# Late second-table gathers, a last batch in two parts, and whole output quarters in one transfer

## The chip, the core and the metric

The kernel runs on one core of a Trainium2 chip. A core has TensorE (PE, matmul; PEld is its weight load), VectorE (DVE), ScalarE (ACT), GpSimd (POOL) and SyncE (SP), each with its own instruction stream, and 16 DMA engines that they share. PE writes its results to eight banks. The metric is the device time of one execution in microseconds, as the median of a few runs.

## The reference

Two transformer blocks run over 256 tokens of width 2048. The change touches only the end of the second one, a layer of 16384 single-neuron experts that are picked by product keys. For each token and each of 8 heads, 16 experts are chosen by two sorted key searches; `expert_u` and `expert_v` are the two tables of 16384 rows of 2048 floats.

```python
def token_block(args):
    xb, idx, g = args
    u = jnp.take(expert_u, idx, axis=0)
    a = jnp.einsum('thkd,td->thk', u, xb)
    hid = jax.nn.gelu(a) * g
    vsel = jnp.take(expert_v, idx, axis=0)
    return jnp.einsum('thk,thkd->td', hid, vsel)

x = x + peer(rms_norm_2(x, norm2_g[l]), ...)   # token_block over blocks of 128 tokens
```

## The kernel before

Everything up to the expert layer is left alone by the change. In the expert layer the tokens are two tiles of 128. Experts whose first key is 88 or more are computed densely from whole panels, which are all used up by about 2930 us. The others are gathered row by row with indirect DMAs: a gather moves, for one slot of one head, a row of 2048 floats for each of 128 tokens, and leaves out tokens whose expert is a dense one. There are 256 gathers from the first table (u0 to u255, line 585) and 256 from the second (v0 to v255, line 601). Four consecutive gathers of each make one of 64 batches g; batches 32 to 63 belong to the second tile.

What a batch goes through, engine by engine:

- POOL issues all gathers, in program order, in the loop at line 608. First-table rows go to one of 5 buffers `u_slot` (`gather_u` waits for the dot that read the buffer five gathers ago, `dot_ready`), second-table rows to one of 7 buffers `v_slot` (`gather_v` waits for the matmuls of the gather seven before it, `v_used`). In step k the loop issues u(k) and then v(k-4); after u255 it issues v252 to v255.
- DVE takes the dot product of a gathered row and the token in two halves (`dot`, line 1706), adds the halves of a batch (`dots_summed`, line 1718), and later multiplies gelu by the gate (`hidden`, line 1756). In the loop at line 1798 `hidden(g - 1)` stands behind the first dot of batch g.
- ACT takes gelu of a batch (line 1097) and then spreads the four products of every token into 16 blocks of 32 x 32, four for each of the four second-table gathers (`spreads`, line 1050), which are the weights of PE's next matmuls.
- PE takes, for each second-table gather k, its spread and its rows and adds into one of the four banks of a tile (`adds`, line 2291): a quarter q of the tile's 32 x 4 block. It waits for `spread_ready` and for the gather's landing. The last batch, 63, finishes one quarter with each of its four gathers and signals `acc_done`.
- DVE copies a finished quarter from its bank to `out_row` (`result`, line 1796): the first tile's four quarters at the end of batch 61, the second tile's four at the very end.
- SP sends `out_row` to HBM (line 484). A quarter lies as 128 partitions of 512 floats, and partitions c*32 to c*32+31 are columns c*512 and on of 32 output rows. SP sends it as four transfers of 32 partitions.

Of the kernel before, what the change touches and what calls it, by code (L numbers as in the profile page):

```python
# [24 lines left out]
TT = T // 128  # L25
# [8 lines left out]
PH, TOPK, NKEYS = 8, 16, 128  # L34
SLOTS = PH * TOPK
# [90 lines left out]
SHRINK = 2.0 ** -16  # L126
# [43 lines left out]
def v_panels_in(i):  # L170

    return range(3 * (i - 34) // 2, min(DENSE, 3 * (i - 33) // 2)) if i >= 34 and 3 * (i - 34) // 2 < DENSE else range(0)


class Counts:
# [39 lines left out]
def two_layers(nc, stream, dense_u, columns, x, meta, b_out, g_mix_post, g_ffn, g_ffn_post, g_norm1, g_norm2, w_forget,  # L215
               forget_bias, group_w, keys, expert_u, expert_v, out):
    f32, f32r, u32 = mybir.dt.float32, mybir.dt.float32r, mybir.dt.uint32
    ACT, ALU, AX = mybir.ActivationFunctionType, mybir.AluOpType, mybir.AxisListType


    K, Q = 1024, 32
# [17 lines left out]
    ident = keep("s_ident", [128, 128])  # L239
# [87 lines left out]
    NU, NV, NW, NH, BATCH, LAG = 5, 7, 4, 4, 4, 4  # L327
    ROUTES, GROUPS = TT * PH, TOPK // BATCH
# [10 lines left out]
    out_row = place("s_out_row", [128, TT, D], S + 24 * K)  # L339
# [43 lines left out]
    with ExitStack() as ctx:  # L383
# [68 lines left out]
        @block.sync  # L452
        def _(sp):
            sp.dma_start(meta_sb[:, :], meta).then_inc(meta_loaded, 16)
            for t in range(TT):
                sp.dma_start(xres[:, t, :], x[t * 128:(t + 1) * 128, :]).then_inc(x_loaded[t], 16)
            sp.dma_start(cols[:, :], columns).then_inc(cols_loaded, 16)
            for s in range(4):
                sp.dma_start(raw[s][:, :], stream[s]).then_inc(raw_loaded[s], 16)
            panels = stream.rearrange("(q s) p n -> q s p n", s=4)  # L460
            with sp.Fori(1, NPANELS // 4) as q:
                for s in range(4):


                    sp.wait_ge(panel_used, q * 4 + (s - 4 + 1 + 1))
                    sp.dma_start(raw[s][:, :], panels[bass.ds(q, 1), s].rearrange("a p n -> (a p) n"))\
                        .then_inc(raw_loaded[s], 16)
            for d in range(NE, 2 * DENSE):
                if d == DENSE:
                    sp.wait_ge(panel_used, NPANELS + 1 + DENSE)  # L470
                    sp.dma_start(xn_late[:, :], put_by[0]).then_inc(xn_back, 16)
                    sp.dma_start(xres_late[:, :], put_by[1]).then_inc(xres_back, 16)
                if d < NE + 2:
                    sp.wait_ge(split_ready, NSPLITS - 3 + d - NE)
                else:
                    sp.wait_ge(panel_used, NPANELS + 1 + d + 1 - 2)
                src = dense_u[d] if d < DENSE else expert_v[(SPARSE + d - DENSE) * NKEYS:(SPARSE + d - DENSE + 1) * NKEYS, :]
                r = (d - NE) % 2
                sp.dma_start(raw[r][:, :], src).then_inc(raw_loaded[r], 16)
            for t in range(TT):  # L480
                for q in range(4):
                    sp.wait_ge(out_ready, 4 * t + q + 1)
                    for c in range(4):
                        sp.dma_start(out[t * 128 + q * Q:t * 128 + (q + 1) * Q, c * 512:(c + 1) * 512],
                                     out_row[c * Q:(c + 1) * Q, t, q * 512:(q + 1) * 512]).then_inc(stored, 16)
            sp.wait_ge(stored, 16 * 16 * TT)


        @block.gpsimd
        def _(pool):  # L490
            n = Counts()
# [112 lines left out]
            gather_u(0)  # L604
            gather_v(0)
            gather_v(1)
            for k in range(1, ROUTES * TOPK + LAG):
                if k < ROUTES * TOPK:
                    gather_u(k)
                for first in {4: (2, 3), 5: (4, 5), 6: (6,)}.get(k, ()):  # L610
                    gather_v(first)
                if k >= LAG + NV:
                    gather_v(k - LAG)


        @block.scalar
        def _(act):
# [420 lines left out]
            v_indices(2)  # L1038


            def spreads(g):

                act.wait_ge(hid_ready, g + 1)
                if g == 0:
                    act.wait_ge(panel_used, NPANELS + 1 + 1)
                wait(act, v_used, 4 * (g + 1 - NW))
                for q in range(4):
                    for s in range(4):
                        own = slice(q * Q, (q + 1) * Q)
                        ins = act.activation(spread[g % NW][s * Q:(s + 1) * Q, q, :], ident[own, own], ACT.Copy,  # L1050
                                             scale=hid[g % NH][own, s:s + 1])
                    ins.then_inc(spread_ready, 1)

            def dense_hidden(d):

# [29 lines left out]
            for g in range(ROUTES * GROUPS):  # L1085
                if g == 18:
                    for t in range(TT):
                        slots_transposed(t)
                if g:
                    spreads(g - 1)  # L1090
                    for d in u_panels_in(g - 1):
                        dense_hidden(d)
                for f in token_fours_in(g):
                    if f % 4 < 2:
                        one_keys(f)
                act.wait_ge(dots_added, g + 1)
                act.activation(gelu[g % NH][:, :], adot[g % NH][:, :], ACT.Gelu_apprx_tanh, scale=1.0 / SHRINK).then_inc(gelu_ready, 1)
                if route_in(g):
                    gate_exps(route_in(g))
                    v_indices(route_in(g))  # L1100
            spreads(ROUTES * GROUPS - 1)


        @block.vector
        def _(dve):
# [603 lines left out]
                                                   accum_out=halfdot[g % NH][:, h * BATCH + s:h * BATCH + s + 1])  # L1709
                ins.then_inc(dot_ready, 1)  # L1710

            def dots_summed(g):

                dve.wait_ge(dot_ready, (g + 1) * BATCH)
                if g >= NH:
                    dve.wait_ge(gelu_ready, g - NH + 1)
                two = halfdot[g % NH]
                dve.tensor_tensor(adot[g % NH][:, :], two[:, 0:BATCH], two[:, BATCH:], ALU.add).then_inc(dots_added, 1)

            def one_keys_2(m):  # L1720

# [27 lines left out]
                dve.tensor_tensor(some, some, bank[b][:, 0:GATE_TOKENS * DENSE].rearrange("p (t g) -> p g t", t=GATE_TOKENS), ALU.mult)\  # L1749
                    .then_inc(bank_empty[b], 1)  # L1750

            def hidden(g):

                th, j = four_of(g)
                dve.wait_ge(gelu_ready, g + 1)
                dve.tensor_tensor(hid[g % NH][:, :], gelu[g % NH][:, :], gate_kept[th][:, j * BATCH:(j + 1) * BATCH], ALU.mult)\  # L1756
                    .then_inc(hid_ready, 1)


            dve.wait_ge(iota_ready, 1)  # L1760
# [32 lines left out]
            def result(t, q):  # L1793

                dve.wait_ge(acc_done, 4 * t + q + 1)
                dve.tensor_copy(out_row[:, t, q * 512:(q + 1) * 512], bank[4 * t + q][:, :]).then_inc(out_ready, 1)

            for g in range(ROUTES * GROUPS):
                for turn in range(BATCH):
                    dot(g * BATCH + turn)  # L1800
                    if turn == 0 and g:
                        hidden(g - 1)
                        if route_in(g - 1):
                            gates_softmax(route_in(g - 1))
# [9 lines left out]
                            one_keys_late(f // 4)  # L1814
                    if g == 32 and turn < 2:
                        gated(T // GATE_TOKENS - 2 + turn)
                dots_summed(g)
                if g == 61:
                    for q in range(4):
                        result(0, q)  # L1820
            hidden(ROUTES * GROUPS - 1)
            for q in range(4):
                result(1, q)

# [575 lines left out]
```

## Time and profile before

| | us |
|---|---|
| median of three runs | 3002.79 |
| lowest and highest | 2999.24, 3002.88 |
| the profiled execution | 3000.82 |
| its span | 2998.8 |
| PE busy | 2758.8 |
| DVE busy | 1923.8 |
| ACT busy | 1178.2 |
| POOL busy | 652.6 |

The span runs from the first to the last instruction of the profiled execution; about 2 us of that execution's time lie outside it. The page's forty slices are 75 us each. Views of the trace name an operation by its line, its engine and its tiles, and give the idle time before it in brackets with what ended it. The chain of waits is followed back from the last instruction, at each step to what released it.

### The profile page before, as it was taken

Reading aid. Unit: us, or ns where it says so; the run is one execution under the profiler, and the core shown is the slowest. Engines: PE = TensorE matmul, PEld = TensorE weight load, DVE = VectorE, ACT = ScalarE, POOL = GpSimd, SP = SyncE. Lnnn points to the kernel's source line nnn. Section 1 sums busy time; section 2 is a strip of 40 time slices with the busy share of each in tenths; the row PEclk is TensorE's granted clock in tenths of the full one; section 3 lists DMA queues with packets and bytes.
Section 4 is the critical chain, followed back from the end, with each engine's and each line's share of the span. In section 5 each row is a group of like instructions: output and inputs, shape, how many; then the busy total and the mean of one; then the engine's idle time right before and its main releaser. Section 6 shows DMA issues by size and latency. Waiting matters only on the chain.

```text
span 2998.8 us, 45605 instructions
## 1 busy us (share of the span) xinstructions
PE 2758.8 (92%) x17100; PEld 2069.8 (69%) x17100; DVE 1923.8 (64%) x3184; ACT 1178.2 (39%) x2298; POOL 652.6 (22%) x568
## 2 busy tenths in 40 slices
PE   8999999999999997999999999999977887887884
PEld 7886788888888887989999889777754432222230
DVE  6888566556656565455444558987869875555555
ACT  1003443333334344435334444655556542222223
POOL 0000000000000000040000002444447664444453
PEclk9999999999999998999999999999977678998996
DMA  6333545555555553443455657999999999999998
GB/s 244 141 141 106 206 161 187 184 194 182 191 187 187 190 184 129 155 155 141 177 186 184 239 200 259 363 418 409 416 383 396 390 416 417 415 413 394 414 407 319
DMA packets 131299, 785.52 MB, mean 262 GB/s; under 512 B 34631, under 2 KB 34631, under 8 KB 35847
## 3 DMA queue, kind: packets, MB, share of 16 engines
q1 hardware_dynamic: 55424, 393.68, 35.6%
q0 software_dynamic: 75712, 389.74, 32.3%
q8 instruction: 94, 1.54, 0.2%
q14 instruction: 69, 0.56, 0.1%
HBM read 940.23 MB, written 4.19 MB: 315 GB/s over the span
## 4 chain that ended last, share of the span: by engine, by line
PE 57%; DMA 19%; DVE 12%; issue 7%; ACT 3%; POOL 2%; DVEq 1%; POOLq 0%; SPq 0%; ACTq 0%
DMA s_u<-in_expert_u,s_u_index 15%; PE bank L1847 10%; PE bank L1841 10%; PE bank L1842 10%; PE bank L1843 10%; PE bank L1848 5%; PE bank L1937 4%; PE bank L2240 4%; DVE s_u L1706 4%; DMA s_v<-in_expert_v,s_v_index 3%; PE bank L2291 2%; POOL s_u L585 2%; DVE s_cacc L1217 2%; DVE s_w_lo L1128 1%; DVE s_yrow L1390 1%
## 5 line engine op out<-in xcount | busy, mean ns | idle before, releaser
L1128 DVE TENSOR_TENSOR s_w_lo<-s_raw,s_w_hi 128x2048 fp32r<-128x2048 f32 x258 | 592.6, 2297 | 578.0 <-ACT s_w_hi L628 577.6
L628 ACT ACTIVATE s_w_hi<-s_raw 128x2048 fp32r<-128x2048 f32 x256 | 490.4, 1916 | 751.7 <-PE bank L1843 476.3
L1847 PE MATMUL bank<-s_a,s_w_hi 128*128 128x512 f32 x1408 | 493.8, 394 | 3.4 <-DVE s_w_lo L1128 3.2
L1706 DVE CUSTOM_DVE_ANT_0 s_u<-s_u,s_xn_late 128x1024 f32<-128x1024 f32 x256 | 303.7, 1224 | 244.0 <-DMA s_u<-in_expert_u,s_u_index 217.1
L2291 PE MATMUL bank<-s_v,s_spread 128*32 128x512 f32 x2048 | 310.3, 715 | 152.0 <-DMA s_v<-in_expert_v,s_v_index 121.6
L1050 ACT ACTIVATE s_spread<-s_ident,s_hid 32x32 f32<-32x32 f32 x1024 | 325.7, 318 | 205.0 <-DVE s_hid L1756 175.8
L1848 PE MATMUL bank<-s_a,s_w_lo 128*128 128x256 f32 x1408 | 394.8, 280 | 0.0
L585 POOL DMA_INDIRECT s_u<-in_expert_u,s_u_index x256 | 292.5, 1142 | 432.1 <-DVE s_halfdot L1706 267.9
L601 POOL DMA_INDIRECT s_v<-in_expert_v,s_v_index x256 | 309.9, 1211 | 191.7 <-PE bank L2291 109.6
L1706 DVE CUSTOM_DVE_ANT_0 s_u<-s_u,s_xn 128x1024 f32<-128x1024 f32 x256 | 303.8, 1224 | 56.0 <-DMA s_u<-in_expert_u,s_u_index 49.6
L1841 PE MATMUL bank<-s_a,s_w_hi 128*128 128x256 f32 x1152 | 325.3, 282 | 4.1 <-DVE s_a L1152 2.4
L1842 PE MATMUL bank<-s_a,s_w_hi 128*128 128x256 f32 x1152 | 324.6, 282 | 0.0
L1843 PE MATMUL bank<-s_a,s_w_lo 128*128 128x256 f32 x1152 | 324.2, 281 | 0.0
L1847 PEld LDWEIGHTS bank<-s_a,s_w_hi 128*128 128x128 f32 x1408 | 264.3, 188 | 66.5 <-DVE s_w_lo L1128 6.4
L2291 PEld LDWEIGHTS bank<-s_v,s_spread 128*32 128x32 f32 x2048 | 64.1, 119 | 345.0 <-issue 267.0
L2250 PE MATMUL bank<-s_raw,s_ha 128*32 128x512 f32 x2560 | 298.9, 616 | 0.2 <-DMA s_raw<-in_expert_v 0.2
L2240 PE MATMUL bank<-s_xnt,s_raw 128*128 128x256 f32 x1184 | 264.8, 382 | 2.9 <-ACT s_ha L1060 1.7
L1848 PEld LDWEIGHTS bank<-s_a,s_w_lo 128*128 128x128 f32 x1408 | 264.6, 188 | 0.4
L2240 PEld LDWEIGHTS bank<-s_xnt,s_raw 128*128 128x128 f32 x1184 | 222.1, 190 | 59.6 <-issue 28.2
L1937 PE MATMUL bank<-s_a_f,s_raw 128*128 128x272 f32 x1024 | 235.2, 393 | 2.1 <-DVE s_a_f L1185 1.4
L2250 PEld LDWEIGHTS bank<-s_raw,s_ha 128*32 128x32 f32 x2560 | 97.6, 115 | 201.6 <-issue 195.7
L1841 PEld LDWEIGHTS bank<-s_a,s_w_hi 128*128 128x128 f32 x1152 | 218.0, 189 | 8.5 <-issue 4.4
(321 smaller groups left out, 3821.8 us busy)
## 6 DMA issues: line engine op xcount, KB each, us to landing
s_raw<-in_stream SPq DMA_DIRECT2D x292, 1024.0 KB, 4.7
s_raw<-in_expert_v SPq DMA_DIRECT2D x40, 1024.0 KB
s_raw<-in_dense_u SPq DMA_DIRECT2D x37, 1024.0 KB
s_u<-in_expert_u,s_u_index POOLq DMA_INDIRECT x256
s_v<-in_expert_v,s_v_index POOLq DMA_INDIRECT x256
s_panel_early<-in_dense_u POOLq DMA_DIRECT2D x3, 1024.0 KB, 11.4
s_xres<-in_x SPq DMA_DIRECT2D x2, 1024.0 KB, 5.9
out<-s_out_row SPq DMA_DIRECT2D x32, 64.0 KB
```

The lines of the kernel that those rows point to most:

```text
L628: act.activation(w_hi[s % 2][:, :], raw[s][:, :], ACT.Copy).then_inc(hi_ready, 1)
L1128: dve.tensor_tensor(w_lo[s % 2][:, :], raw[s][:, :], w_hi[s % 2][:, :].bitcast(f32), ALU.subtract)\
L1706: ins = dve.tensor_tensor_reduce(out=u_slot[k % NU][:, half], in0=u_slot[k % NU][:, half], in1=xn_late[:, half] if t else xn[:, 0, half], ...
L1841: pe.matmul(dst, left[0], right[0], start=start, stop=False)
L1842: pe.matmul(dst, left[0], right[1], start=False, stop=False)
L1843: return pe.matmul(dst, left[1], right[0], start=False, stop=stop)
L1847: pe.matmul(dst, left[0], both, start=start, stop=False)
L1848: return pe.matmul(dst[:, 0:T], left[1], both[:, 0], start=False, stop=stop)
L1937: ins = pe.matmul(bank[c][:, 0:L], raw[c % 4][:, k * 128:(k + 1) * 128], a_f[:, k, :], start=k == 0, stop=k == KT - 1)
L2240: ins = pe.matmul(bank[b][:, 0:T], source[:, k * 128:(k + 1) * 128], xnt[:, k, 0:T], start=k == 0, stop=k == KT - 1)
L2250: ins = pe.matmul(bank[4 * t + q][c * Q:(c + 1) * Q, :], ha[:, d, t * 128 + q * Q:t * 128 + (q + 1) * Q], raw[r][:, c * 512:(c + 1) * 512] ...
L2291: ins = pe.matmul(bank[4 * t + q][c * Q:(c + 1) * Q, :], spread[g % NW][:, q, :], v_slot[k % NV][:, c * 512:(c + 1) * 512], start=False, s ...
```

## The change

Three things change. First, POOL's loop: up to step 247 it stays at u(k), v(k-4). In steps 248 to 255 a second-table gather is issued only in every second step (`v_steps_in`), so v244, v245 and v246 follow u249, u251 and u253, and v247 to v255 all follow u255. Second, the last batch: `hidden(62)` stands ahead of the first dot of batch 63 instead of behind it. The sum, gelu and product of batch 63 are made for its first three slots before the last dot and for the fourth after it, and its 16 spread blocks come as twelve and then four; `spread_ready` is signalled with the last four. Third, SP sends an output quarter as one transfer instead of four, with the 4 x 32 x 512 arrangement on the HBM side.

```diff
+def v_steps_in(k):
+    if k < SLOTS * TT - 8:
+        return range(k - 4, k - 3)
+    first = SLOTS * TT - 12 + (k - SLOTS * TT + 8) // 2
+    if k == SLOTS * TT - 1:
+        return range(first, SLOTS * TT)
+    return range(first, first + k % 2)
...
-                    for c in range(4):
-                        sp.dma_start(out[t * 128 + q * Q:t * 128 + (q + 1) * Q, c * 512:(c + 1) * 512],
-                                     out_row[c * Q:(c + 1) * Q, t, q * 512:(q + 1) * 512]).then_inc(stored, 16)
-            sp.wait_ge(stored, 16 * 16 * TT)
+                    sp.dma_start(out[t * 128 + q * Q:t * 128 + (q + 1) * Q, :].rearrange("p (c n) -> c p n", c=4),
+                                 out_row[:, t, q * 512:(q + 1) * 512]).then_inc(stored, 16)
+            sp.wait_ge(stored, 16 * 4 * TT)
...
-            for k in range(1, ROUTES * TOPK + LAG):
-                if k < ROUTES * TOPK:
-                    gather_u(k)
+            for k in range(1, ROUTES * TOPK):
+                gather_u(k)
...
-                if k >= LAG + NV:
-                    gather_v(k - LAG)
+                for own in v_steps_in(k):
+                    if own >= NV:
+                        gather_v(own)
...
+            def last_spreads(g):
+                act.wait_ge(hid_ready, g + 1)
+                act.wait_ge(v_used, 4 * (g + 1 - NW))
+                for q in range(4):
+                    for s in range(3):
+                        one_spread(g, q, s)
+                act.wait_ge(dots_added, g + 2)
+                gelu_of(g, slice(3, 4))
+                act.wait_ge(hid_ready, g + 2)
+                for q in range(4):
+                    one_spread(g, q, 3).then_inc(spread_ready, 1)
...
-                act.activation(gelu[g % NH][:, :], adot[g % NH][:, :], ACT.Gelu_apprx_tanh, scale=1.0 / SHRINK).then_inc(gelu_ready, 1)
+                gelu_of(g, slice(0, 3 if g == ROUTES * GROUPS - 1 else 4))
...
-            spreads(ROUTES * GROUPS - 1)
+            last_spreads(ROUTES * GROUPS - 1)
...
+            last = ROUTES * GROUPS - 1
             for g in range(ROUTES * GROUPS):
+                if g == last:
+                    hidden(g - 1)
                 for turn in range(BATCH):
+                    if g == last and turn == 3:
+                        dots_summed(g, 0, 3)
+                        hidden(g, 0, 3)
                     dot(g * BATCH + turn)
-                    if turn == 0 and g:
+                    if turn == 0 and 0 < g < last:
                         hidden(g - 1)
...
-                dots_summed(g)
+                if g == last:
+                    dots_summed(g, 3, 4)
+                else:
+                    dots_summed(g)
...
-            hidden(ROUTES * GROUPS - 1)
+            hidden(last, 3, 4)
```

On POOL the last twelve gathers stand as follows, before and then now. `s_u_133` to `s_u_137` are the five first-table buffers, `s_v_138` to `s_v_144` the seven second-table buffers, and the number behind an index names the head.

```order
L585 DMA s_u_135<-in_expert_u,s_u_index_190 128x2048
L601 DMA s_v_141<-in_expert_v,s_v_index_205 128x2048
L585 DMA s_u_136<-in_expert_u,s_u_index_190 128x2048
L601 DMA s_v_142<-in_expert_v,s_v_index_205 128x2048
L585 DMA s_u_137<-in_expert_u,s_u_index_190 128x2048
L601 DMA s_v_143<-in_expert_v,s_v_index_205 128x2048
L585 DMA s_u_133<-in_expert_u,s_u_index_190 128x2048
L601 DMA s_v_144<-in_expert_v,s_v_index_205 128x2048
L601 DMA s_v_138<-in_expert_v,s_v_index_206 128x2048
L601 DMA s_v_139<-in_expert_v,s_v_index_206 128x2048
L601 DMA s_v_140<-in_expert_v,s_v_index_206 128x2048
L601 DMA s_v_141<-in_expert_v,s_v_index_206 128x2048
```

```order
L610 DMA s_v_139<-in_expert_v,s_v_index_204 128x2048
L594 DMA s_u_137<-in_expert_u,s_u_index_190 128x2048
L594 DMA s_u_133<-in_expert_u,s_u_index_190 128x2048
L610 DMA s_v_140<-in_expert_v,s_v_index_204 128x2048
L610 DMA s_v_141<-in_expert_v,s_v_index_205 128x2048
L610 DMA s_v_142<-in_expert_v,s_v_index_205 128x2048
L610 DMA s_v_143<-in_expert_v,s_v_index_205 128x2048
L610 DMA s_v_144<-in_expert_v,s_v_index_205 128x2048
L610 DMA s_v_138<-in_expert_v,s_v_index_206 128x2048
L610 DMA s_v_139<-in_expert_v,s_v_index_206 128x2048
L610 DMA s_v_140<-in_expert_v,s_v_index_206 128x2048
L610 DMA s_v_141<-in_expert_v,s_v_index_206 128x2048
```

Before, u252 to u255 alternate with v248 to v251 and four second-table gathers follow; now nine follow u255 (`s_u_133`, index 190), from v247 to v255.

On DVE the end of batch 63 stands as follows, before and then now. An ISA row that writes `s_u` is half a dot, one with `s_halfdot` alone reads its sum.

```order
L1706 ISA s_u_137,s_halfdot_226<-s_u_137,s_xn_late 128x1024
L1706 ISA s_halfdot_226 128x1
L1706 ISA s_u_133,s_halfdot_226<-s_u_133,s_xn_late 128x1024
L1706 ISA s_halfdot_226 128x1
L1706 ISA s_u_133,s_halfdot_226<-s_u_133,s_xn_late 128x1024
L1706 ISA s_halfdot_226 128x1
L1718 TENSOR_TENSOR s_adot_230<-s_halfdot_226 128x4
L1756 TENSOR_TENSOR s_hid_238<-s_gelu_234,s_gate_kept_222 128x4
L1796 COPY s_out_row<-bank 128x512 x4
```

```order
L1748 TENSOR_TENSOR s_adot_230<-s_halfdot_226 128x3
L1787 TENSOR_TENSOR s_hid_238<-s_gelu_234,s_gate_kept_222 128x3
L1736 ISA s_u_133,s_halfdot_226<-s_u_133,s_xn_late 128x1024
L1736 ISA s_halfdot_226 128x1
L1736 ISA s_u_133,s_halfdot_226<-s_u_133,s_xn_late 128x1024
L1736 ISA s_halfdot_226 128x1
L1748 TENSOR_TENSOR s_adot_230<-s_halfdot_226 128x1
L1787 TENSOR_TENSOR s_hid_238<-s_gelu_234,s_gate_kept_222 128x1
L1827 COPY s_out_row<-bank 128x512 x4
```

The sum and the product are made twice, for three slots ahead of the last dot and for one behind it; the four copies stay last.

On SP the end of the program, the last panel loads and the output, stands as follows, before and then now.

```order
L479 DMA s_raw_65<-in_expert_v 128x2048
L479 DMA s_raw_66<-in_expert_v 128x2048
L479 DMA s_raw_65<-in_expert_v 128x2048
L484 DMA out<-s_out_row 32x512 x32
L383 UNCONDITIONAL_BRANCH
```

```order
L489 DMA s_raw_65<-in_expert_v 128x2048
L489 DMA s_raw_66<-in_expert_v 128x2048
L489 DMA s_raw_65<-in_expert_v 128x2048
L493 DMA out<-s_out_row 4x32x512 x8
L393 UNCONDITIONAL_BRANCH
```

Thirty-two transfers of the form 32x512 become eight of the form 4x32x512, in the same place.

## Rows read from the trace of the kernel before

**Rows 1.** The page's forty slices: DMA busy tenths and GB/s.

```profile
DMA  6333545555555553443455657999999999999998
GB/s 244 141 141 106 206 161 187 184 194 182 191 187 187 190 184 129 155 155 141 177 186 184 239 200 259 363 418 409 416 383 396 390 416 417 415 413 394 414 407 319
```

**Rows 2.** Chain of waits, last 50 us: start us, us, what.

```profile
2950.33 19.74 DMA s_u<-in_expert_u,s_u_index
...
2973.95 1.98 PE bank L2291 x8
...
2976.76 14.89 DMA s_v<-in_expert_v,s_v_index
...
2991.79 1.10 PE bank L2291 x8
...
2992.91 0.69 DVE s_out_row L1796
```

**Rows 3.** Busy us by stretch, engine by engine (instructions); last: PEclk, DMA share, GB/s.

```profile
2936.00:2976.00 40.00, 17.40 (x76) 2.17 (x80) 25.48 (x49) 13.85 (x45) 19.47 (x18) 0.54 1.00 404
...
2976.00:2980.00 4.00, 1.54 (x12) 0.19 (x8) 2.38 (x4) 1.82 (x6) 0.99 (x1) 0.92 0.76 279
2980.00:2984.00 4.00, 1.35 (x8) 0.00 (x0) 2.24 (x3) 0.00 (x0) 0.00 (x0) 0.51 0.31 129
2984.00:2988.00 4.00, 3.76 (x20) 0.73 (x24) 0.46 (x4) 3.26 (x11) 0.00 (x0) 0.50 0.06 27
```

**Rows 4.** DMA view of 2984:2988, all packets.

```profile
DMA packets 20, 0.11 MB, mean 27 GB/s; under 512 B 7, under 2 KB 7, under 8 KB 7
```

**Rows 5.** Timeline of DVE, batches 62 and 63: start us, us, what [idle before].

```profile
2965.37 1.23 DVE L1706 CUSTOM_DVE_ANT_0 s_u<-s_u,s_xn_late 128x1024 f32<-128x1024 f32 x1 [2.60 <-issue]
...
2970.09 1.23 DVE L1706 CUSTOM_DVE_ANT_0 s_u<-s_u,s_xn_late 128x1024 f32<-128x1024 f32 x1 [2.14 <-DMA s_u<-in_expert_u,s_u_index]
...
2972.39 0.16 DVE L1756 TENSOR_TENSOR s_hid<-s_gelu,s_gate_kept 128x4 f32<-128x4 f32 x1
...
2977.50 1.23 DVE L1706 CUSTOM_DVE_ANT_0 s_u<-s_u,s_xn_late 128x1024 f32<-128x1024 f32 x1 [1.67 <-DMA s_u<-in_expert_u,s_u_index]
...
2981.76 1.23 DVE L1706 CUSTOM_DVE_ANT_0 s_u<-s_u,s_xn_late 128x1024 f32<-128x1024 f32 x1 [1.88 <-DMA s_u<-in_expert_u,s_u_index]
```

**Rows 6.** Timeline of POOL: the issues of u255 and of v255.

```profile
2963.61 0.99 POOL L585 DMA_INDIRECT s_u<-in_expert_u,s_u_index  x1 [2.57 <-DVE s_halfdot L1706]
...
2976.76 0.99 POOL L601 DMA_INDIRECT s_v<-in_expert_v,s_v_index  x1 [4.58 <-PE bank L2291]
```

**Rows 7.** Timeline of ACT (gelu of batch 62) and of PE (matmuls of v251 to v255).

```profile
2967.99 0.20 ACT L1097 ACTIVATE s_gelu<-s_adot 128x4 f32<-128x4 f32 x1 [8.21 <-DVE s_adot L1718]
...
2984.08 1.93 PE L2291 MATMUL bank<-s_v,s_spread 128*32 128x512 f32 x8 [2.74 <-DMA s_v<-in_expert_v,s_v_index]
2986.17 4.82 PE L2291 MATMUL bank<-s_v,s_spread 128*32 128x512 f32 x24 [0.15 <-ACT s_spread L1050]
2991.79 1.06 PE L2291 MATMUL bank<-s_v,s_spread 128*32 128x512 f32 x8 [0.80 <-DMA s_v<-in_expert_v,s_v_index]
```

**Rows 8.** Timeline of SP, the second tile's output, and of DVE, its first copy.

```profile
2988.17 0.69 DVE L1796 COPY s_out_row<-bank 128x512 f32<-128x512 f32 x1 [3.41 <-PE bank L2291]
2988.89 8.21 SPq L484 DMA_DIRECT2D out<-s_out_row  x16
```

**Rows 9.** DMA view, output queue q1: first tile in 2952:2968, second in 2989.6:2999 (with slices).

```profile
q1 hardware_dynamic: 768, 1.05, 17.7%
...
DMA  4510055540918172919191818281918281810000
...
q1 hardware_dynamic: 768, 1.05, 42.4%
```

## What I expected, written before the run

> **What bounds the kernel now.** I read the page's slices first, then the chain of waits at the end, then short stretches. From about 1900 us to the end the DMA engines are busy throughout (mean share 0.8 to 0.9 and more, 360 to 418 GB/s but for the last slice) [rows 1]. The chain of waits ends with the last second-table gather: POOL issues v255 at 2976.76, it lands 14.89 us later, then come one set of matmuls, one copy and the output [rows 2]. Taken at its word, the chain says that v255 was issued too late, because its slot waited for the matmuls at 2973.95, and these for a first-table landing at 2970.07 [rows 2].
>
> The stretches say otherwise. From 2936 to 2976 the share is 1.00 at 404 GB/s, so the 16 engines move about 25 GB/s each, while PE is busy for 17.4 of the 40 us. It falls to 0.31 in 2980:2984 and to 0.06 in 2984:2988, where 27 GB/s are left [rows 3, 4]. A share of 0.06 is one engine of 16, still at its full rate. The other fifteen drained at about 2981: 0.31 x 16 x 4 us is 19.8 us of engine time, less 4 for the one, over 15. So one engine is some 10 us behind the others, and every gather waits for its part.
>
> Was that engine ever out of work near the end? When POOL issued u255 at 2963.61, u251 had not been consumed (its dot starts at 2965.37); when it issued v255 at 2976.76, the dots of u254 (2977.50) and u255 (2981.76) had not begun [rows 5, 6]. Issues ran ahead of that engine's landings all the time. So the landing at 2991.66 follows from how many rows the slowest engine has to move, and not from when v255 was issued.
>
> **The change part by part.**
>
> *Order of the gathers.* The same 512 gathers are issued. Eight move: v244 now follows u249 instead of u248, v245 to v247 pass 2, 3 and 4 first-table gathers, v248 to v250 pass 3, 2 and 1, v251 none. On the slowest engine this exchanges places in a queue that does not run dry, so v255's landing changes by 0. The new wait is POOL's: after u255 come nine second-table gathers, and v253 to v255 wait for the matmuls of v246 to v248. Behind a waiting gather stand only the rest of the nine, and PE waits for them. The cover is the queue: when v246 lands, u254, u255 and v247 to v252 are still to come. Eight gathers at 1.9 us (v251's matmuls start at 2984.08, v255 lands at 2991.66, four gathers between [rows 2, 7]) are some 15 us against about 1 us of POOL for an issue [rows 6]. Each microsecond without this cover would cost one at the end. I take 0.
>
> *Last batch in two parts.* Batch 62's product now comes ahead of dot 252. Gelu is ready at 2968.19, the product was made at 2972.39 behind a dot that waited for its row until 2970.09 [rows 5, 7], so it comes 4.2 us earlier. Batch 63's spreads were late: PE's 24 matmuls at 2986.17 were released by ACT [rows 7]. With u255 four places further ahead (4 x 1.9 = 7.6 us) they are ready before v252 lands. Then PE takes each gather as it lands; but v255's matmuls waited for the DMA already (0.80 us idle [rows 7]), so the gain on the path is 0. ACT gets one gelu more and DVE a sum and a product more (0.16 to 0.20 us each) plus two waits for gelu; they stand before dots 252 and 255, far ahead of v252. A loss is possible: PE's eight matmuls took 1.06 us at the end, but 1.93 in sparser work [rows 7], so up to +0.9.
>
> *Output.* This is where the sum is made. Before, each quarter (128 x 512) went out in four transfers of 32 rows of 2 KB. SP issued the last 16 in 8.21 us, 0.51 each, until 2997.10, though the last copy ended at 2993.60 [rows 2, 8]. So 3.5 us of SP's issuing lie on the path. Now there are four issues, and that term goes. What is late next is the transfer itself. SP's row gives the old form as 32x512 and the new one as 4x32x512; every other SP row in this program has 128 outermost, or 16. The old form used more than a quarter of the engines: its packets filled 42.4% of 16 engines [rows 9]. No row shows an outermost count of 4. The bounds: its 128 rows go over 16 engines, 8 each, or over 4, one per outermost index, 32 each. I take four, since a share per outermost index is what the form asks for.
>
> A sentence of the Trainium skill stands behind this: "DMA: Bandwidth & Descriptors", section "Why a DMA increments its semaphore by 16 and not by 1", says that the outermost dimensions of both sides set how many engines take part, the largest count up to 16 that divides both. By that rule 4 and 128 give four engines, and on SP's queue always the same four. No run here shows it yet.
>
> Price of a 2 KB row on one engine: in 2952:2968, between gathers, 512 of them took 17.7% of 16 x 16 us, so 0.088 us; at the end 42.4% of 16 x 9.4 us, so 0.125 [rows 9]. I take 0.088, the price with work queued, and keep 0.125. A quarter is then 32 x 0.088 = 2.8 us on four engines, the second tile's four quarters 11.3 us. The first tile's quarters, at about 2950, put 128 rows on each of the four instead of 32 (+8.5 us) and take 2.8 us from each of the other twelve.
>
> *Sum*, slowest engine among the twelve: last gather 2991.66 - 2.8 = 2988.8. v252 lands three gathers sooner, 2983.1; matmuls 1.9, copy 0.7, issue and start about 1: the first quarter's packets begin at 2986.8, and 11.3 us of them end at 2998.1. The four engines' own work gives 2981 + 8.5 + 11.3 = 3000.8, or 2998.0 if the 2.8 us by which the queue runs sooner count in full. I take 2999.0 for the last packet. The last slices before the end are empty, 0.9 us [rows 9], so the span is 2999.9: **1.1 us over the 2998.8 profiled**. That execution took 3000.82 in all; the median of the three runs is 3002.79 (2999.24 to 3002.88). So 3003.9. At 0.125 the burst is 16 us: +5.8, 3008.6.
>
> **The rivals.**
>
> *All sixteen engines.* The first tile's load is spread as before, the last gather lands at 2991.66, the last copy ends at 2993.60, the issue at 2994.1; from the end of the last issue to the end of the span it was 1.7 us, plus six more rows per engine at 0.088 to 0.125, 0.6: 2996.4, which is -2.4, and 3000.4. For it: all transfers of before spread widely. Against: none had this form.
>
> *The chain is right.* If the landing follows the issue, batch 62's product 4.2 us earlier brings v255 4.2 us earlier, with the 2.4 above -6.6: 2996.2. Against: rows 3 to 6.
>
> *The slowest engine is one of the four* (the slower side). Its gathers then end 8.5 us later, 3000.2, and the first three quarters' rows alternate with its last gathers, up to 8.5 more; after that matmuls, copy, issue, 2.8 of rows and 0.9: about 7. The middle is 3011.4, +12.6, so 3015.4 (3011.2 to 3019.7). It decides as soon as the four include that engine, one case in four when four engines are used. No row names the engine.
>
> *The merge saves SP nothing*, if an issue of the new form takes four times as long: the page has no such row; 16 x 0.51 would be kept at most, and the time stays at 3002.8. I count it with the forecast.
>
> **How the numbers follow.** Four engines 0.62: 0.47 without the slowest engine (forecast 3003.9) and 0.15 with it. Sixteen engines 0.30. The chain right 0.08. Range: 2997 to 3009 holds the forecast with its dearer row and the sixteen engines with the spread of the runs, and leaves out 0.15 above and about half of 0.08 below. What a measurement of this kernel can tell from no change is about 0.2%, 6 us: faster 0.05 (the chain right, in part), slower 0.16, the same 0.79.
>
> **What would show it.** The first table's last dot some 7 us earlier against the last second-table landing, nine second-table issues in a row on POOL, and a landing of v255 that is not earlier for being issued otherwise: the order is worth nothing. Four SP issues in the last stretch instead of 16. Over the last 9 us the output queue's share at 25% of the engines or under, near 4 x 25 GB/s, with packets back to back: four engines; short bursts above 25% and an end about 3 us after the last copy: sixteen. v255 landing near 2988.8: the first tile's rows left the slowest engine; after 2999: they fell on it. I am wrong in the main step if v255 lands much earlier without that, with DMA share 1.00 until later than 2977, and wrong on the price if a quarter takes far from 2.8 us.

## The result and the profile after

| | before | after |
|---|---|---|
| median, us (runs) | 3002.19 (22) | 3005.70 (22) |
| lowest and highest | 2999.12, 3004.93 | 3003.55, 3009.69 |
| ratio, 95% interval | | 1.0014 [1.0008, 1.0019] |
| the profiled execution | 3000.82 | 3004.03 |
| its span | 2998.8 | 3002.0 |

The changed kernel is 3.5 us slower, 0.14%. The forecast of 3003.9 had the direction and 1.1 us of it. The span of the profiled execution grew by 3.2 us. The stretches of the kernel after (busy us by engine, then PEclk, DMA share, GB/s) answer [rows 3]:

```profile
2944.00:2948.00 4.00, 1.93 (x8) 0.23 (x8) 3.02 (x7) 0.00 (x0) 1.69 (x2) 0.50 0.80 299
2948.00:2952.00 4.00, 1.93 (x8) 0.23 (x8) 3.97 (x8) 0.21 (x1) 1.27 (x2) 0.50 0.89 323
2952.00:2956.00 4.00, 1.08 (x8) 0.20 (x8) 3.80 (x9) 2.35 (x8) 1.41 (x2) 0.50 0.73 261
...
2980.00:2984.00 4.00, 3.87 (x24) 0.58 (x16) 0.00 (x0) 0.00 (x0) 0.98 (x1) 0.65 0.90 336
2984.00:2988.00 4.00, 2.38 (x20) 0.37 (x16) 0.99 (x2) 0.00 (x0) 0.00 (x0) 1.00 0.38 154
2988.00:2992.00 4.00, 2.13 (x16) 0.37 (x16) 1.78 (x3) 0.00 (x0) 0.00 (x0) 1.00 0.24 67
2992.00:2996.00 4.00, 0.00 (x0) 0.00 (x0) 0.00 (x0) 0.00 (x0) 0.00 (x0) 0.63 0.26 102
2996.00:3000.00 4.00, 0.00 (x0) 0.00 (x0) 0.00 (x0) 0.00 (x0) 0.00 (x0) 0.50 0.26 100
```

Read it from below. The last 8 us hold nothing but the output, at a share of 0.26 and 100 GB/s: four engines of 16, at 25 GB/s each. Further up, two things changed places. In 2944 to 2956, where the DMA engines had been full [rows 3], the share is 0.73 to 0.89; and in 2980:2984, where before only a third of the engines had work, it is 0.90. Most engines now have gaps in the middle and work to do at the end.

The end of the chain of waits (start us, us, what) answers [rows 2]:

```profile
2957.11 11.61 DMA s_u<-in_expert_u,s_u_index
...
2980.39 9.44 DMA s_v<-in_expert_v,s_v_index
...
2989.96 1.10 PE bank L2331 x8
...
2991.09 0.69 DVE s_out_row L1827
```

v255 is issued 3.6 us later than before and lands at 2989.83 (2980.39 + 9.44), 1.8 us earlier. The last copy ends at 2991.78, but the span at 3002.0. The view of what SP waits for (line, releaser: us, times, longest) and the DMA view of 2989.6 to 3002 (slices of 0.31 us in tenths and in GB/s, then the output queue: packets, MB, share) say what fills those 10.2 us:

```profile
SPq L393 <- DMA out<-s_out_row: 9.2, 1, 9.2
```

```profile
DMA  1322222222222222222222222222222221000000
GB/s 66 53 53 79 73 86 92 106 99 106 106 92 99 106 106 99 106 106 106 92 99 106 106 99 106 106 92 99 106 106 99 106 86 59 20 26 26 13 0 0
...
q1 hardware_dynamic: 514, 1.02, 22.2%
```

SP has issued everything and waits 9.2 us for the stores. The rows run back to back, at some 100 GB/s, where before they came in bursts with pauses [rows 9]. One of them costs 0.222 x 16 x 12.4 / 514 = 0.086 us.

### The profile page after: what moved, and what is told of

Same layout as the page of the kernel before. It is cut to its first block, busy times and chain, and to the rows that moved or that the text cites. A ratio compares the mean times of both kernels' runs of the same rounds, so it can differ in the third digit from the quotient of the medians.

```text
span 3002.0 us, 45585 instructions
## 1 busy us (share of the span) xinstructions
PE 2760.0 (92%) x17100; PEld 2068.9 (69%) x17100; DVE 1924.1 (64%) x3186; ACT 1178.3 (39%) x2299; POOL 657.1 (22%) x568
## 3 DMA queue, kind: packets, MB, share of 16 engines
q8 instruction: 94, 1.54, 0.2%
## 4 chain that ended last, share of the span: by engine, by line
PE 57%; DMA 19%; DVE 11%; issue 7%; ACT 3%; POOL 2%; DVEq 1%; POOLq 0%; SPq 0%; ACTq 0%
DMA s_u<-in_expert_u,s_u_index 15%; PE bank L1887 10%; PE bank L1881 10%; PE bank L1882 10%; PE bank L1883 10%; PE bank L1888 5%; DMA s_v<-in_expert_v,s_v_index 4%; PE bank L1977 4%; DVE s_u L1736 3%; PE bank L2280 3%; PE bank L2331 2%; DVE s_cacc L1247 2%; POOL s_u L594 1%; DVE s_w_lo L1158 1%; PE bank L2320 1%
## 5 line engine op out<-in xcount | busy, mean ns | idle before, releaser
L1887 PEld LDWEIGHTS bank<-s_a,s_w_hi 128*128 128x128 f32 x1408 | 264.3, 188 | 66.4 <-DVE s_w_lo L1158 6.4
L1977 PEld LDWEIGHTS bank<-s_a_f,s_raw 128*128 128x128 f32 x1024 | 194.4, 190 | 43.0 <-issue 3.1
```

The lines of the kernel that those rows point to most:

```text
L1887: pe.matmul(dst, left[0], both, start=start, stop=False)
L1977: ins = pe.matmul(bank[c][:, 0:L], raw[c % 4][:, k * 128:(k + 1) * 128], a_f[:, k, :], start=k == 0, stop=k == KT - 1)
```

## A common mark

Executions drift by up to some 4 us before the end, more than is to be explained. So I compare kernels from a mark that the change leaves in place: the start of the first tile's four copies on DVE, which stands between 2948.1 and 2952.7 in the kernels below. The timelines of DVE have it, of before and after:

```profile
2934.79 1.23 DVE L1706 CUSTOM_DVE_ANT_0 s_u<-s_u,s_xn_late 128x1024 f32<-128x1024 f32 x1 [1.73 <-DMA s_u<-in_expert_u,s_u_index]
...
2949.59 2.48 DVE L1796 COPY s_out_row<-bank 128x512 f32<-128x512 f32 x4
```

```profile
2933.87 1.22 DVE L1736 CUSTOM_DVE_ANT_0 s_u<-s_u,s_xn_late 128x1024 f32<-128x1024 f32 x1 [1.74 <-DMA s_u<-in_expert_u,s_u_index]
...
2948.67 2.48 DVE L1827 COPY s_out_row<-bank 128x512 f32<-128x512 f32 x4
```

A dot that waited for its row stands 14.80 us ahead of the copies in both, so the mark is sound. From it v255 lands at +42.06 before and at +41.16 after (2989.83 - 2948.67). All kernels, in us. Each experiment has 11 runs (the two halves 5), and its ratio is to runs of the kernel before that were taken beside it (medians 3002.86, 3002.81 and 3001.86), not to 3002.19. The last three columns come from one profile each:

| kernel | median | ratio to before [95%] | v255 lands, from the mark | last copy's end to span's end | span's end, from the mark |
|---|---|---|---|---|---|
| before | 3002.19 | | 42.1 | 5.2 | 49.2 |
| after | 3005.70 | 1.0014 [1.0008, 1.0019] | 41.2 | 10.2 | 53.3 |
| output as before | 3000.50 | 0.9997 [0.9988, 1.0006] | 42.7 | 3.5 | 49.0 |
| merged output alone | 3004.75 | 1.0005 [0.9996, 1.0014] | 39.3 | 9.4 | 50.7 |
| first tile merged | 3001.24 | 0.9998 [0.9989, 1.0007] | 41.7 | 5.4 | 49.1 |
| second tile merged | 3005.30 | 1.0009 [1.0000, 1.0018] | 42.7 | 8.7 | 54.0 |
| 128 outermost | 2999.98 | 0.9989 [0.9980, 0.9998] | 43.3 | 2.9 | 48.2 |
| two halves | 3026.21 | 1.0080 [1.0066, 1.0094] | 45.1 | 25.1 | 73.0 |
| two queues | 2999.12 | 0.9989 [0.9980, 0.9998] | 42.6 | 2.9 | 47.4 |
| two queues, old order, old last batch | 2996.86 | 0.9980 [0.9971, 0.9989] | 39.4 | 2.9 | 44.3 |
| two queues, late order alone | 2999.29 | 0.9991 [0.9982, 1.0000] | 42.4 | 2.9 | 47.2 |
| two queues, split last batch alone | 2997.01 | 0.9981 [0.9972, 0.9990] | 39.4 | 3.0 | 44.3 |
| two queues, no first-tile stores | 2996.82 | 0.9981 [0.9972, 0.9990] | 39.6 | 2.9 | 44.4 |

## Experiments: which part costs the time

**The output as before.** The merged transfer is undone in the kernel after:

```diff
-sp.dma_start(out[...].rearrange("p (c n) -> c p n", c=4), out_row[:, t, ...])
+for c in range(4):
+    sp.dma_start(out[..., c * 512:(c + 1) * 512], out_row[c * Q:(c + 1) * Q, t, ...])
```

> The kernel after, with the output as before: 16 transfers of 32x512 for each tile. Left of the change are the order of the late gathers and the last batch in two parts. My theory (one lagging DMA engine sets the end, so the order is worth nothing, and only the merged output made the kernel after 3.5 us longer): the same time as before within 1 us, about 3002, a ratio of 1.000; v255 is issued some 3.6 us later than before and lands within 1 us of 2991.7. Rival (the order holds the last landing back, or brings it forward): v255's landing moves with its issue. If the order or the two parts cost the 3.5 us, this kernel is as long as the one after, about 3005.7; if the chain of waits was right about the issue, it is about 4 us shorter than before, 2998.

The ratio is 0.9997, so the loss is gone with the merged output. In the chain v255 is issued at 2980.41, 3.65 us later than before (4.2 from the mark), and lands at 2991.80, 0.1 us later (0.7 from the mark):

```profile
2980.41 11.39 DMA s_v<-in_expert_v,s_v_index
```

A landing does not follow its issue here: the chain's story of a gather issued too late is refuted, as the forecast said.

**The merged output alone**, on the kernel before:

> The kernel before, with the merged output alone: each quarter one transfer of 4x32x512. My theory (the merged transfer runs on four of the 16 DMA engines and makes all of the loss): as long as the kernel after, +2 to +4 us over before, 3004 to 3006; the last 11 to 13 us at a share of about a quarter of the DMA engines and 100 GB/s. Rival (the order and the two parts make the loss): the same as before or up to 2.4 us shorter, since SP's 3.5 us of issuing go.

The ratio is 1.0005; the interval reaches from none to all of the loss of the kernel after, so the traces must decide. From the mark v255 lands 2.7 us sooner than before, as priced (2.8). The mark, v255 in the chain, and the stretches of this kernel's end:

```profile
2949.33 2.48 DVE L1795 COPY s_out_row<-bank 128x512 f32<-128x512 f32 x4
```

```profile
2973.84 14.83 DMA s_v<-in_expert_v,s_v_index
```

```profile
2980.00:2984.00 4.00, 2.68 (x12) 0.43 (x16) 1.55 (x6) 2.23 (x8) 0.00 (x0) 0.50 0.27 110
...
2992.00:2996.00 4.00, 0.00 (x0) 0.00 (x0) 0.00 (x0) 0.00 (x0) 0.00 (x0) 0.70 0.26 101
```

The four-engine burst is here too, but in 2980:2984 the other engines are through, as before. Its span is 3000.0. The forecast's sum, which put 0 on the other two parts, was 2999.9. From the mark it loses 1.5 us (50.7 against 49.2), where the sum had 1.1. So the sum holds for this part alone, and the kernel after loses 2.6 us more (53.3 against 50.7). The merged output doesn't make all of the loss, as had been expected here, and the parts do not add up. Alone, the late order and the split batch lose nothing at the end (49.0 against 49.2).

**One tile merged, the other not**, both on the kernel after:

```diff
+if t == 0:   # in the other kernel: t == 1
     sp.dma_start(out[...].rearrange("p (c n) -> c p n", c=4), out_row[:, t, ...])
+else:
+    for c in range(4): ...
```

> The kernel after, but only the first tile's quarters are merged; the second tile's go out in four transfers each, as before. My theory: the four DMA engines that carry the merged rows are not the lagging one, so at about 2950 they take 2.8 us of rows from the lagging engine and v255 lands 1 to 2.8 us earlier than before, about 2989 to 2990.5; the end is that of before less that much: a ratio of 0.999 to 0.9997. Rival (the lagging engine is one of the four): v255 lands some 8 us later and the kernel is about 8 us longer. Rival (the first tile's rows matter to nothing): the same as before.

> The kernel after, but only the second tile's quarters are merged; the first tile's go out in four transfers each, as before. My theory (the loss is the burst of 512 rows on four DMA engines at the end, about 13 us from the first packet): v255 lands as before, within 1 us of 2991.7, the first packets come at about 2989, the end at about 3002: +2 to +4 us over before, 3004.5 to 3006.5. If the kernel after also loses by the first tile's rows (they hold back the four engines, so the burst starts behind their gathers), this kernel is some 1 to 3 us shorter than the kernel after. Rival (the second tile's merge is harmless): the same as before.

With the second tile merged alone the end is as late as in the kernel after (54.0 against 53.3 from the mark): the burst is the loss, and the first tile's merge neither adds to it nor takes much away. With the first tile alone v255 gains only 1.0 us over the output as before, not the 2.7 that the same merge gains with the old order. Nor does the end come 1 to 2.8 us sooner, as had been expected (49.1 against 49.2 before): the last landings come closer together, and SP's 16 issues are the tail again. Timelines of SP, of the kernel with the first tile merged and of the one with two queues (below):

```profile
2986.82 8.74 SPq L498 DMA_DIRECT2D out<-s_out_row  x16
```

```profile
2987.86 6.36 SPq L498 DMA_DIRECT2D out<-s_out_row  x8
```

The first ends at 2995.56, 3.65 us after the last copy; the second, with ACT issuing the other half, 0.8 us after it.

## Experiments: how many engines a transfer gets

**A count of 128 outermost, and a count of 2.**

```diff
-out[t * 128 + q * Q:t * 128 + (q + 1) * Q, :].rearrange("p (c n) -> c p n", c=4)
+out.rearrange("t (c n) -> (t c) n", c=4)[(4 * t + q) * 128:(4 * t + q + 1) * 128, :]
```

> The kernel after, still with one transfer for a quarter, but as a plain 128x512 transfer whose outermost count is 128: the same bytes in the same 2 KB rows, written to other places of the output (a quarter's 128 rows of 512 lie one behind the other, so the output's arrangement is not the reference's). My theory: it runs on all 16 DMA engines, so nothing is left of the long burst and SP's issuing tail is gone as well: the output ends about 3 us after the last copy, and the kernel is 2 to 3 us shorter than before, 2999 to 3000, and 5 to 6 us shorter than the kernel after. Rival (one merged transfer costs the time whatever its outermost count, because it starts late or its rows are slow): the same as the kernel after, about 3005.7.

```diff
-sp.dma_start(out[...].rearrange("p (c n) -> c p n", c=4), out_row[:, t, ...])
+for h in range(2):
+    sp.dma_start(out[..., h * 1024:(h + 1) * 1024].rearrange("p (c n) -> c p n", c=2),
+                 out_row[h * 64:(h + 1) * 64, t, ...])
```

> The kernel after, with each quarter in two transfers of 2x32x512 in place of one of 4x32x512. My theory (the outermost count of 4 is what puts the rows on four engines): a count of 2 puts them on two, 64 rows for each transfer's half of a quarter's 128 per engine, 256 rows for a tile: 256 x 0.084 = 21.5 us. The first tile's rows then make these two engines the last ones (2981 + 18.8 = 2999.8), v255 lands at about 2999 or later, and the end is at about 3021 to 3025: +20 to +26 us over before; the share of the DMA engines at the end is 0.13 and about 50 GB/s. Rival (four engines by something else than the outermost count, as the number of rows or the queue): as the kernel after, +3.5, at a share of 0.25.

The DMA view of the plain transfers, 2992 to 2998.6 (slices of 0.165 us):

```profile
DMA  1049995000029998100000000002999700000000
GB/s 50 0 186 410 447 385 211 0 25 37 25 87 385 410 397 323 37 25 25 12 0 0 0 0 0 0 0 112 410 397 397 273 0 0 0 0 0 0 0 0
```

and the stretches of the two halves:

```profile
3000.00:3004.00 4.00, 0.00 (x0) 0.00 (x0) 0.00 (x0) 0.00 (x0) 0.00 (x0) 0.50 0.13 51
3004.00:3008.00 4.00, 0.00 (x0) 0.00 (x0) 0.00 (x0) 0.00 (x0) 0.00 (x0) 0.50 0.13 51
```

The same 2 KB rows run at 400 GB/s with 128 outermost (a quarter takes some 0.8 us), at 100 with 4, and at 51 with 2: all engines, four, two. The output's tail after the last copy is 2.9, 10.2 and 25.1 us. By the Trainium skill ("DMA: Bandwidth & Descriptors", section "Why a DMA increments its semaphore by 16 and not by 1") the outermost dimensions of both sides set the number, as the largest count up to 16 that divides both; these three kernels agree with it. One number of the expectation failed: with two engines v255 was to land at 2999 or later and landed at 2993.85, so the first tile's rows held the gathers back by far less than their 18.8 us. The end held: +23.4 us, a span of 3021.8.

## Experiments: what the late order costs

**Two queues**: the kernel after, with the first tile merged, and the second tile's transfers of 32x512 shared by SP and ACT.

```diff
+for c in range(2):       # SP, second tile
+    sp.dma_start(out[..., c * 512:(c + 1) * 512], out_row[c * Q:(c + 1) * Q, 1, ...])
...
+for q in range(4):       # ACT, behind its last spreads
+    act.wait_ge(out_ready, 4 + q + 1)
+    for c in range(2, 4): act.dma_start(out[..., c * 512:(c + 1) * 512], out_row[c * Q:(c + 1) * Q, 1, ...])
```

> The kernel after, with the first tile's quarters merged and the second tile's in transfers of 32x512 again, of which SP issues two for each quarter and ACT, which is idle by then, the other two. My theory: the first tile's rows leave the lagging engine, v255 lands 1 to 2.8 us earlier than before (2989 to 2990.5); the rows of the end run on all 16 engines; each of the two queues issues 8 transfers of 0.5 us beside the other, so the issuing ends about 1 us after the last copy and the span about 3.3 us after it: 3 to 4 us shorter than before, 2998.5 to 3000, and 1 to 2 us shorter than with SP alone. Rival (the issuing was no limit, or ACT's issues cost more than SP's): the same as with SP alone, 1 to 2 us shorter than before.

**The same output on the kernel before:**

> The kernel before, with the output alone as in the experiment with two queues: the first tile's quarters merged, the second tile's in transfers of 32x512, two of each quarter from SP and two from ACT. Order of the gathers and last batch are those of before. My theory (order and last batch are worth nothing): within 1 us of the experiment with two queues on top of the kernel after, 2998.5 to 3000; v255 is issued some 3 us earlier than there and lands at the same time. It can lose up to 1 us where ACT's spreads, which stand before its issues, release three gathers' matmuls at once. Rival (the order or the last batch is worth something once the output is off the path): 2 us or more apart.

The tail is 2.9 us in both, and the first came to the time expected, though v255 landed only at 2991.47 (0.5 us later than before, from the mark). But the kernel with the old order ends 3.1 us sooner from the mark, and its v255 lands 3.2 us sooner (39.4 against 42.6). "Order and last batch are worth nothing" failed. The mark and v255 with the old order, on DVE's timeline and in the chain:

```profile
2948.14 2.48 DVE L1805 COPY s_out_row<-bank 128x512 f32<-128x512 f32 x4
```

```profile
2972.64 14.89 DMA s_v<-in_expert_v,s_v_index
```

The next two kernels separate the two parts, and a third takes the first tile's stores away. The first diff sets POOL's loop in the one kernel against that in the other; the comments say which last batch each has.

```diff
-for k in range(1, ROUTES * TOPK + LAG):   # old order, split last batch
+for k in range(1, ROUTES * TOPK):         # late order, old last batch
```

> The kernel before with the two-queue output (first tile's quarters merged, second tile's 32x512 transfers shared by SP and ACT), and with the late order of the gathers alone; the last batch is that of before. Measured from the start of the first tile's copies, v255 landed at +39.4 us with the old order and this output, at +42.6 with both the late order and the split last batch. My theory (the late order leaves 15 engines short of work in 2940 to 2960, so they end some 3 us later, and the four that carry the first tile's merged rows become the last): v255 lands at +41 to +43, the share of the DMA engines falls under 0.9 in 2944 to 2956 and is near 0.9 still in 2980 to 2984; the time is 2 to 3 us over that of the old order, 2998.5 to 3000. Rival (the split last batch cost it): v255 at +39.4 and 2996.9.

> The same two-queue output with the old order of the gathers, and the last batch in two parts as the only other change. My theory (the split is worth nothing on the path): v255 lands at +39.4 us after the start of the first tile's copies, as with the unsplit batch, and the time is within 1 us of that, 2996 to 2998. Rival (the split batch cost the time): v255 at +41 to +43 and 2998.5 to 3000. If the three quarters before the last go out earlier and this counts, it is up to 1 us shorter.

```diff
-if t == 0: sp.dma_start(...)   # first tile's stores
```

> The kernel after with the two-queue output for the second tile, and without the stores of the first tile (its half of the output is not written). The late order and the split batch stay. My theory (with the late order the four engines of the first tile's merged rows set the last landings; the lagging engine alone would be ready earlier): without those rows v255 lands at +39 to +40.5 us after the start of the first tile's copies, 2 to 3 us earlier than with them (+42.6), and the time is about 2997. Rival (the late order loses on the lagging engine itself, which runs dry): v255 stays at +41.5 to +43, and the time at 2999.

The copies on DVE's timeline and v255 in the chain, first of the late order alone, then of the kernel without the first tile's stores:

```profile
2949.89 2.48 DVE L1815 COPY s_out_row<-bank 128x512 f32<-128x512 f32 x4
```

```profile
2980.78 11.50 DMA s_v<-in_expert_v,s_v_index
```

```profile
2952.68 2.48 DVE L1834 COPY s_out_row<-bank 128x512 f32<-128x512 f32 x4
```

```profile
2980.85 11.40 DMA s_v<-in_expert_v,s_v_index
```

All three came out as the theory said. The split batch is worth nothing (+39.40; 2997.0 against 2996.9 us). The late order alone costs 3.0 us (+42.39). Without the first tile's stores, the late order costs nothing (+39.57). So the merged first tile loses nothing by itself, and the late order at most the 0.7 us seen with the output as before; together they lose 3.0. The stretches show the link, of the late order and of the old one, both with two queues:

```profile
2952.00:2960.00 8.00, 1.94 (x8) 0.20 (x8) 7.75 (x15) 5.01 (x16) 3.24 (x3) 0.50 0.80 291
2980.00:2984.00 4.00, 2.96 (x16) 0.42 (x16) 0.00 (x0) 0.59 (x2) 0.99 (x1) 0.76 0.94 341
2984.00:2988.00 4.00, 2.67 (x16) 0.65 (x16) 0.00 (x0) 0.00 (x0) 0.00 (x0) 0.67 0.43 175
```

```profile
2952.00:2960.00 8.00, 3.71 (x20) 0.73 (x24) 5.71 (x11) 5.09 (x16) 5.08 (x4) 0.68 0.96 364
2980.00:2984.00 4.00, 3.85 (x20) 0.73 (x24) 0.34 (x4) 3.39 (x11) 0.00 (x0) 0.50 0.24 101
```

With the late order DVE is busy for 7.75 of 8 us in 2952:2960: first-table rows arrive one behind the other, and its dots and the four copies fill it. POOL's next first-table gather waits for a dot, and there is no second-table gather between to issue. On the timeline of POOL that wait, for u253, stands here, first in the late order alone and then in the old order:

```profile
2955.51 1.23 POOL L599 DMA_INDIRECT s_u<-in_expert_u,s_u_index  x1 [3.89 <-DVE s_halfdot L1725]
```

```profile
2953.76 1.70 POOL L589 DMA_INDIRECT s_u<-in_expert_u,s_u_index  x1 [2.59 <-DVE s_halfdot L1715]
```

u253 goes out 5.62 us behind the mark in both, so the late order doesn't bring the first table's rows forward here. By then the old order has also issued v246, v247 and v248, and the late order none of them: those are the rows that the engines miss.

So the share falls to 0.80, and the work that the engines miss then comes at the end, at 0.94 in 2980:2984 where the old order has 0.24. The lagging engine hardly cares (0.7 us with the output as before), since it has a queue throughout. But the others used to be some 10 us ahead of it, and now have less: v255 is their last work too, and is issued some 4 us later, which leaves about 6 (an estimate). The first tile's merged rows put 8.5 us more on four of them, by the forecast's price. With 10 us to spare that is hidden, with 6 it is not.

The trace settles which engine ended last. It keeps sixteen landing signals for a gather, as many as there are DMA engines. Those of v255 in order of time, in us from the mark, and the time from v254's last signal to v255's:

| kernel | ninth | 13th, 14th, 15th | last | from v254's last |
|---|---|---|---|---|
| before | 31.8 | 32.1, 32.7, 34.6 | 42.1 | 2.52 |
| output as before | 36.8 | 37.4, 37.9, 38.5 | 42.7 | 2.66 |
| two queues, old order, old last batch | 30.3 | 35.8, 36.8, 37.1 | 39.4 | 2.51 |
| two queues, no first-tile stores | 34.2 | 34.5, 34.5, 34.9 | 39.6 | 2.68 |
| two queues, late order alone | 35.7 | 39.5, 39.6, 39.7 | 42.4 | 1.55 |
| after | 36.6 | 38.7, 39.6, 40.9 | 41.2 | 1.54 |

Before, one signal comes 7.5 us behind the fifteenth, as the share of 0.06 had one engine at work: I read a signal as one engine's part. From the ninth to the last there are 10.3 us before and 5.9 with the output as before, so the estimate of 6 is borne out. The merged first tile makes three more signals late, still ahead of the lagging engine's with the old order. In the last two rows the lagging engine is no longer the last one: its step from v254 to v255 is 2.45 to 2.68 us in all eight kernels in which the late order and the first tile's rows on four engines do not meet, and the step is 1.54 to 1.55 in the four in which they do (the two halves left aside). So another engine has become the last, and the kernel without the first tile's stores says that it is one that carries those rows. Why one engine lags in the first place, no run here shows.

## Why the prediction was nearly right, point by point

- **One lagging engine sets v255.** Held: with the output as before, an issue 4.2 us later from the mark moved the landing by 0.7, and the merged first tile gained 2.7 us of 2.8 priced with the old order. It stops being true in the kernel after, where another engine lands last.
- **Order worth 0.** This is the step that failed. Its argument looked at the lagging engine alone, whose queue does not run dry. It missed that the late order eats the lead of the other fifteen, and that the next term of the same sum (first tile's rows, 8.5 us on four of them) was drawn on that lead. (Seven gathers change places, not eight; v251 keeps its own.) The cost is 2.6 us (53.3 against 50.7 from the mark); in the kernel after v255 gains 0.9 instead of 2.8.
- **Last batch worth 0.** Held, by 0.01 us in v255's landing. The possible +0.9 did not come in the kernel after: at the end PE's matmuls took 1.06 us, at a granted clock of 1.00, the upper of its two levels (2.4 GHz), after PE had been busy for 3.87 of the 4 us in 2980:2984. The timelines of ACT and PE:

```profile
2976.18 1.34 ACT L1053 ACTIVATE s_spread<-s_ident,s_hid 32x32 f32<-32x32 f32 x4 [0.23 <-DVE s_hid L1787]
```

```profile
2985.03 1.07 PE L2331 MATMUL bank<-s_v,s_spread 128*32 128x512 f32 x8 [0.79 <-DMA s_v<-in_expert_v,s_v_index]
...
2989.96 1.06 PE L2331 MATMUL bank<-s_v,s_spread 128*32 128x512 f32 x8 [0.47 <-DMA s_v<-in_expert_v,s_v_index]
```

  The spreads are done 7.5 us ahead of v252, and PE takes each gather as it lands, where ACT had released three at once [rows 7]. But the loss did come in three of the experiments with the split batch: v255's matmuls took 1.94 us with the output as before, 1.78 with the second tile merged and 1.94 with the two halves. The first of these, on PE's timeline, ran at a granted clock of 0.50 (1.2 GHz), behind 1.60 us of idle:

```profile
2991.93 1.94 PE L2332 MATMUL bank<-s_v,s_spread 128*32 128x512 f32 x8 [1.60 <-DMA s_v<-in_expert_v,s_v_index]
```

- **Four engines, 0.088 us a row.** Held: share 0.26, and 0.086 us. The rival of all sixteen engines is out. Its price for the tail was good: as a plain transfer with 128 outermost the merged output left 2.9 us behind the last copy (2.8 forecast, 5.2 before). In whole time it gave -2.9 us by the medians and -1.1 from the mark (-2.4 forecast), since that kernel has the late order too.
- **The sum.** The first copy of the second tile was to start at 2985.0 (2983.1 and 1.9 of matmuls) and started at 2986.16; from there to the end were to be 14.9 us and were 15.8. So of the 2.1 us by which the span missed, 1.2 are the late start and 0.9 the rest (from the mark it missed by 3.0, and the start by 2.1). With the merged output alone the copy started at 2985.26 and the span ended 14.7 us later, as summed. So both parts are the late order's: from the mark it starts the copy 1.6 us later, and the rest takes 1.1 us longer.
- **The slowest engine among the four** (+12.6): out, since v255 lands 2.7 us sooner with the old order, not 8 later.

## What to carry to other kernels

Slack is spent once: where two parts of a change each hide behind the same idle time, price them together, since each may be free alone and the pair not. Before merging small stores into one, look at what stands outermost in it; a count of 4 left 10.2 us of stores behind the last copy, the small stores from one queue 3.5 to 5.4, and from two queues 2.9. The best kernel of this study keeps the old order, merges only the tile whose rows lie beside other work, and shares the last issues between SP and ACT: 2996.9 us, 0.9980 [0.9971, 0.9989] of before. With the split batch added it is the same within the noise (2997.0).

## What had not been expected of the hardware

A merge that concentrates rows on four engines can be a gain: with the old order and two queues it took the 2.7 us of rows from the lagging engine, as priced, without a loss elsewhere. ACT's queue issues stores beside SP's at about SP's pace: in the kernel with two queues eight of them took 6.43 us on ACT and 6.36 on SP, copies waited for included.

```profile
2987.86 6.43 ACTq L1140 DMA_DIRECT2D out<-s_out_row  x8
```
